# Selective scan: the first x unit of each group projected two slots ahead, the z rows in slots six and seven

## What is computed

```python
def _ssd_branch(h, w_in, conv_w, conv_b, dt_bias, A, d_skip, norm_w, w_out, h0_f, h0_b, with_out):
    proj = h @ w_in                       # z | x | B | C | dt
    z, rest = proj[..., :D_INNER], proj[..., D_INNER:]
    xbc = silu(_dwconv(rest[..., :CONV_DIM], conv_w, conv_b))      # five taps along the tokens
    xs, bm, cm = ...                      # x: 4 groups x 8 heads x 64; B, C: 4 groups x 128
    dt = softplus(rest[..., CONV_DIM:] + dt_bias)
    y_f, s_f = _ssd_scan(xs, dt_f, A[0], bm, cm, h0_f, with_out)   # chunks of 128 tokens
    y_b, s_b = _ssd_scan(flip(xs), flip(dt_b), A[1], flip(bm), flip(cm), h0_b, with_out)
    y = y_f + flip(y_b) + d_skip * xs
    gy = _rms_norm(y * silu(z), norm_w)   # per group of 512 channels
    return gy @ w_out, s_f, s_b
```

## Time and profile before

| | |
|---|---|
| median of 3 runs | 1860.78 us (1860.24 to 1864.98) |
| the profiled execution | 1859.74 us |
| its span, first to last instruction | 1857.9 us, and 1.8 us around it |
| mean granted PE clock | 0.994 of 2.4 GHz |
| PE, DVE, ACT, POOL busy | 97%, 61%, 49%, 5% of the span |
| first block of projections | 654.2 to 697.4 us of the span |
| round 0, 1, 2 | 697.4 to 761.4, to 827.8, to 893.2 us |
| experts | from about 1000 us to the end |

### The profile page before, as it was taken

One profiled execution on the slowest core, in us unless ns is written; L12 is line 12 of the kernel. 1 busy time (PEld: TensorE's weight loads), 2 busy tenths in 40 slices (PEclk: granted clock), 3 DMA queues, 4 the chain that ended last, 5 costly groups with the idle time before them and its releaser, 6 DMA issues.

```text
span 1857.9 us, 25616 instructions
## 1 busy us (share of the span) xinstructions
PE 1795.4 (97%) x10135; PEld 1316.4 (71%) x10136; DVE 1131.3 (61%) x1453; ACT 917.6 (49%) x1436; POOL 100.7 (5%) x81
## 2 busy tenths in 40 slices
PE   6989999999999999899999999999999999999997
PEld 5976788888888887687888566665666666655563
DVE  3266476765657797688867565565555555555644
ACT  3235573222246646577756455444454445444433
POOL 1000000000000123323300000000000000000000
PEclk9999999999999999999999999999999999999999
DMA  9466215666355532122259999999999999999995
GB/s 355 146 212 243 91 46 182 211 196 201 139 193 193 164 94 69 37 78 68 92 190 355 386 390 407 409 412 414 410 407 411 412 413 409 409 412 412 413 407 239
DMA packets 182459, 498.22 MB, mean 268 GB/s; under 512 B 10348, under 2 KB 62908, under 8 KB 167996
## 3 DMA queue, kind: packets, MB, share of 16 engines
q1 hardware_dynamic: 181760, 495.93, 70.6%
q10 hardware_dynamic: 571, 0.57, 0.1%
HBM read 495.42 MB, written 1.05 MB: 267 GB/s over the span
## 4 chain that ended last, share of the span: by engine, by line
PE 77%; DVE 8%; DMA 5%; ACT 4%; SPq 3%; issue 2%; POOL 0%; ACTq 0%; DVEq 0%; POOLq 0%
PE bank L991 12%; PE bank L992 11%; PE bank L993 11%; PE bank L1681 9%; PE bank L1673 4%; PE bank L1256 4%; PE bank L1258 4%; PE bank L1257 4%; DMA raw<-in_moe_gu_w_dram 3%; SPq L854 2%; DVE ar L3045 2%; PE bank L1356 2%; PE bank L1357 2%; PE bank L1358 2%; SPq L849 1%
## 5 line engine op out<-in xcount | busy, mean ns | idle before, releaser
L2685 DVE TENSOR_TENSOR lo<-raw,hi 128x1024 fp32r<-128x1024 f32 x182 | 216.9, 1222 | 171.1 <-ACT hi L1975 169.0
L2666 DVE TENSOR_TENSOR lo<-raw,hi 128x1024 fp32r<-128x1024 f32 x172 | 212.8, 1243 | 146.8 <-ACT hi L1955 144.5
L1955 ACT ACTIVATE hi<-raw 128x1024 fp32r<-128x1024 f32 x156 | 164.7, 1059 | 259.1 <-PE bank L1258 172.7
L1975 ACT ACTIVATE hi<-raw 128x1024 fp32r<-128x1024 f32 x182 | 187.0, 1057 | 146.5 <-DMA raw<-in_moe_gu_w_dram 55.5
L991 PE MATMUL bank<-hi,xg_t 128*128 128x512 f32 x448 | 182.3, 407 | 3.4 <-ACT ar L2488 1.4
L992 PE MATMUL bank<-lo,xg_t 128*128 128x512 f32 x448 | 175.2, 391 | 0.0
L993 PE MATMUL bank<-hi,xg_t 128*128 128x512 f32 x448 | 174.9, 390 | 0.0
L2685 DVE TENSOR_TENSOR lo<-ar,hi 128x1024 fp32r<-128x1024 f32 x94 | 112.1, 1222 | 90.4 <-ACT hi L1975 89.1
L991 PE MATMUL bank<-hi,hth 128*128 128x512 f32 x400 | 160.1, 400 | 2.0 <-DVE lo L2685 1.9
L992 PE MATMUL bank<-lo,hth 128*128 128x512 f32 x400 | 156.0, 390 | 0.0
L993 PE MATMUL bank<-hi,htl 128*128 128x512 f32 x400 | 155.8, 390 | 0.0
(11 more groups left out here) (400 smaller groups left out, 3328.9 us busy)
## 6 DMA issues: line engine op xcount, KB each, us to landing
raw<-in_moe_gu_w_dram SPq DMA_DIRECT2D x126, 1024.0 KB, 16.0
raw<-in_moe_down_w_dram SPq DMA_DIRECT2D x60, 1024.0 KB, 16.3
ar<-in_moe_gu_w_dram SPq DMA_DIRECT2D x59, 1024.0 KB, 17.9
out_slot<-in_moe_gu_w_dram SPq DMA_DIRECT2D x39, 1024.0 KB, 15.6
ar<-in_moe_down_w_dram SPq DMA_DIRECT2D x33, 1024.0 KB, 16.1
raw<-in_ada_w_dram SPq DMA_DIRECT2D x14, 2048.0 KB, 9.1
raw<-in_ffn_gu_w_dram SPq DMA_DIRECT2D x22, 1024.0 KB, 5.2
raw<-in_ffn_down_w_dram SPq DMA_DIRECT2D x22, 1024.0 KB, 4.9
```

The costliest lines, as they stand in the source:

```text
L1955: A_(hi[:, p % SPL, :], raw[:, slot(u), (p % 2) * PIECE:(p % 2 + 1) * PIECE], ACT.Copy).then_inc(hi_ready, 1)
L1975: A_(hi[:, q % SPL, :], m_raw(i)[:, (q % 2) * PIECE:(q % 2 + 1) * PIECE], ACT.Copy).then_inc(m_hi, 1)
L2666: TT(lo[:, p % SPL, :], raw[:, u, h * PIECE:(h + 1) * PIECE], hi[:, p % SPL, :].bitcast(F32), ALU.subtract).then_inc(done, 1)
L2685: TT(lo[:, q % SPL, :], src[:, (q % 2) * PIECE:(q % 2 + 1) * PIECE], hi[:, q % SPL, :].bitcast(F32), ALU.subtract).then_inc(m_lo, 1)
```

## The change

Nothing is computed differently. For groups 1, 2 and 3 the two pieces of the first x unit move from slots 0 and 1 to slots 8 and 9 of the round (or block) in front. z of group 1 and group 2 goes as two whole units into slots 6 and 7, two pieces in each. ACT takes the first x unit from the banks in slot 0 and not in slot 1, and z in slots 7 and 8 and not in 7 and 9, ahead of `conv_out` in slot 8. DVE's convolutions of the first x unit stand in slots 1 and 2, those of the second in 4 and 5 as before. `used_by` follows. The fillers of slot 9 of the first block and three of four groups of three in slots 7 to 9 of round 0 go away. Round 3 is as it was.

```diff
         def used_by(g, k):
 
+            ahead = max(0, k - 8)
             if g < 0:
-                return 2 * S_GRP + min(k, 6)
-            if g == 0:
-                return 2 * S_GRP + 6 + min(k, 6)
-            a = 2 * S_GRP + 12 + 10 * (g - 1)
-            if g < N_GROUPS - 1:
-                return a + k
-            return a + min(k, 4) + max(0, k - 6)
+                return 2 * S_GRP + min(k, 6) + ahead
+            a = 2 * S_GRP + (8 if g == 0 else 14 + 10 * (g - 1))
+            if g == N_GROUPS - 1:
+                return a - 2 + min(k, 4) + max(0, k - 6)
+            return a + min(max(0, k - 2), 4) + (2 * min(max(0, k - 6), 2) if g > 0 else 0) + (ahead if g < N_GROUPS - 2 else 0)
@@ PE, project(g, k) @@
                 if k < 4:
-                    proj("x", g, k // 2, k % 2)
+                    if g == 0 or k >= 2:
+                        proj("x", g, k // 2, k % 2)
                 elif k < 6:
                     proj("bc", g, 0, k - 4)
-                elif g > 1:
-                    proj("z", g - 1, (k - 6) // 2, k % 2)
-                if k == 9 and g == 0:
-                    fill(bank[2][:, 0:256], 3)
+                elif k < 8:
+                    if g > 1:
+                        for h in range(2):
+                            proj("z", g - 1, k - 6, h)
+                elif g + 1 < N_GROUPS:
+                    proj("x", g + 1, 0, k - 8)
                 if k >= 5:
                     to_tok(g, k - 5)
                 if k == 9:
-                    if g == 0:
-                        fill(bank[2][:, 0:256], 3)
                     cb(g)
@@ PE, scan(g, k) @@
                 project(g + 1, k)
-                if g == 0 and k >= 7 or g == N_GROUPS - 1 and k in (4, 5):
+                if g == N_GROUPS - 1 and k in (4, 5):
                     late_fill(g, 3)
@@ ACT, project(g, k) @@
-                for i in {1: (0, 1), 3: (2, 3), 5: (4, 5), 8: (6, 7)}.get(k, ()):
+                if k in (7, 8) and g > 1:
+                    zs(g - 1, k - 7)
+                for i in {(0 if g > 0 else 1): (0, 1), 3: (2, 3), 5: (4, 5), 8: (6, 7)}.get(k, ()):
                     if i >= 2:
                         conv_out(g, i - 2)
                     if i < 6:
                         conv_in(g, i)
-                if k in (7, 9) and g > 1:
-                    zs(g - 1, (k - 7) // 2)
@@ DVE, project(g, k) @@
-                if 2 <= k <= 7:
-                    conv(g, k - 2)
+                at = (2, 3, 4, 5, 6, 7) if g == 0 else (1, 2, 4, 5, 6, 7)
+                if k in at:
+                    conv(g, at.index(k))
```

## The result

The changed kernel takes **1908.74 us** (median of 4 runs, 1907.61 to 1910.06) where the kernel before takes 1862.43 (1860.24 to 1864.98, 4 runs beside it): a ratio of **1.0256**, with an interval of 1.0244 to 1.0269. Its profiled execution took 1907.61 with a span of 1905.8; against the span before, 1857.9, that is +47.9 us. The mean granted clock fell from 0.994 to 0.982.

A forecast was written before the change was run, and what follows sets the result against it. Slot by slot, PE's own work or the chain of DVE's, ACT's and PE's short steps, whichever ends last, bounds it. 3.7 - 0.2 + 24.2 - 0.2 + 13.5 = 41.0 us on 1859.74 gives 1902, range 1884 to 1914.

The forecast's parts named there:

- The first block: Slots 8 and 9 get two x pieces in place of fillers and waits; start of round 0 +6.0 us.
- the start chain: ACT's queue ahead of `state_out` at a round's start: PE idles some 6 us in round 0, 10 in rounds 1 and 2.
- The waits for z's copy: Rounds 1 and 2: PE's second z unit or next x waits for ACT's copy behind `m_`, three times, 4 to 5 us.
- if L1356 does not wait for L2273: Sign of being wrong: in the changed profile PE's projection is not held by ACT's copy out of bank 0.
- The rest of round 1: Slots 6 to 9: +24.2 us, of it 11 x pieces, 9.6 the two waits, 3.1 their clock.
- the clock term: Low clock after idling: 1.6 us charged for each long wait of PE, 9.9 us in the sum.
- The start of round 1: From round's start to first `yy` 21.4 us, before 21.6: -0.2 us, the whole 11 us saved given back.
- the rest of round 2: Slots 6 to 9: z waits in slot 7, copy, Silu and table load precede `conv_out` in slot 8; +13.5 us.
- (a): Rival: only round starts and added x bind, ACT's z copies come early enough; +14 us, 1875; 7%.
- (b): Rival: faster, x pieces fill PE's gaps at a round's end and the start chain is not exposed; -14 us, 1847; 4%.
- (c): Rival: PE stays cold, the low clock covers more of each restart; 10 to 15 us more, about 1914; 16%.
- (d): Rival: no change, work is only reordered and the waits found are hidden by the queue; 3%.

The follow-up runs named there:

- e10: Kernel before with only the first x unit of groups 1 and 2 moved ahead, z as before; 1868.43 us, ratio 1.0037.
- e8: e7 with PE projecting slot 2's x piece ahead of `late` and `bc`; 1866.19 us, ratio 1.0025.
- e11: e8 with z one piece a slot in round 2 and DVE's convolutions back in slots 2 to 7; 1855.04 us, ratio 0.9964.
- e1: Changed kernel with ACT's two z copies moved from slots 7 and 8 to 6 and 7, Silu left in slot 8; 1886.53 us, ratio 1.0132.
- e9: Changed kernel with 11 fillers (round 0) and 22 (rounds 1 and 2) in PE's wait ahead of `state_lat`; 1902.49 us, ratio 1.0222.
- e3: Changed kernel with 18 fillers (round 0) and 36 (rounds 1 and 2) ahead of `state_lat`, longer than the wait; 1914.73 us, ratio 1.0279.
- e7: e1 with ACT running two `conv_in` and one `state_out` ahead of the first `ce_` at a round's start; 1872.89 us, ratio 1.0063.
- e4: Kernel before with both z pieces of a unit in slots 6 and 7, ACT's copies in 7 and 8, no x moved; 1889.23 us, ratio 1.0149.

## Why the prediction was right, and where it was not

It forecast slower, 1902 us in a range of 1884 to 1914, and 1908.74 was measured. Against the profiled executions it was +41.0 forecast and +47.9 measured.

**The steps that held.** The first block ran 6.4 us longer for 6.0; so close a hit is luck, since that mark scatters by up to 3.5 us. PE waits for `state_out` 5.3 us in round 0 and 10.1 in rounds 1 and 2; the prediction had "some 6" and 10. That e10 gains nothing from a round with an x unit less at its start, and that e8 and e11 save 7 to 9 of the 11 us a round once ACT's and PE's order are changed, shows that the start chain, and not DVE's or ACT's sum, took the gain. The waits for z's copy came three times at 4.5 to 4.9 (4.6 forecast), and e1 shows the copy as their cause although the profile named another. By its letter the prediction's sign of being wrong ("if L1356 does not wait for L2273") was met in that trace; only e1 set it aside. The Silu ahead of `conv_out` in round 2 cost a wait of 6.4 us; in round 1 it was covered by the x piece. The rest of round 1 was 23.6 for 24.2 (the parts that the prediction gives for it in brackets sum to 23.7; its steps give the 24.2). SP, POOL and the experts gave nothing back, as costed.

**The terms that were sized too small** are those of a round's start, and the largest is the clock term, 1.6 us for each long wait, taken from one z piece at 4.45 in place of 2.88. At a round's start the low clock covers `state_lat`, `late` and `bc`, and e9 and e3 put it at 2.4 to 2.5. The start of round 1, from the timelines of after and e9, by its terms: `state_lat` begins 12.56 us after the round's start, forecast 11.9, because the gated multiply on DVE ahead of `seg` took 2.00 us there and 1.23 before (+0.7); from `state_lat` to `yy` at the full clock 8.5 us and not 7.9 (+0.6); the low clock 2.4 and not 1.6 (+0.8). Together +2.1, the whole gap between 23.5 and 21.4. Round 2 has the same +2.2, and round 0, which has no gated multiply, +1.0 of it.

Why that multiply took longer can be read from the traces. Before (first row) it ran alone. In the changed kernel POOL's product (L945) runs beside it:

```profile
763.23 1.23 DVE L3122 TENSOR_TENSOR ar<-ar,raw 128x1024 f32<-128x1024 f32 x1
```

```profile
768.59 2.00 DVE L3123 TENSOR_TENSOR ar<-ar,raw 128x1024 f32<-128x1024 f32 x1
```

```profile
768.46 1.04 POOL L945 TENSOR_TENSOR ar<-ar 128x512 f32<-128x512 f32 x1 [6.12 <-PE bank L1419]
```

POOL waits there for PE's `state_ctx`, which begins 0.6 us after a round's start now that no x piece stands ahead of it, and began at 6.0 before. So the move itself made the two meet, and the prediction, which had POOL's products wait for ACT alone, did not see it. The count over all traces stands at the end. No run moved POOL's product by itself, so the cause rests on that count.

**In the rest of round 2** 1.8 us were missing. Behind the wait of 1.70 us in its slot 6 the prediction left the clock whole, as it had been before. Afterwards it fell there too, as in round 1, and the z piece that starts at 906.75 took 4.44 us where the one at 873.94 of the kernel before took 2.96: 1.5 of the 1.8. That is chance as far as the traces tell, since in e1 the clock stayed whole at the same place. The windows view of PE alone, changed kernel:

```profile
907.00:909.00 2.00, 2.00 (x12) 0.53 0.00 0
909.00:911.00 2.00, 2.00 (x13) 0.62 0.00 0
```

**Sum of the misses:** round 0 +1.6 (0.4 at its start), round 1 +2.1 and -0.6, round 2 +2.2 and +1.8: 7.1, and 41.0 + 7.1 = 48.1.

**The rivals.** (a), only starts and added x bind, with 1875: its condition, the copy ahead of `m_`, is what e1 makes, and e1 takes 1886.5, +24.8 for +14. The rest of round 1 is then +11.0, as (a) has it. What it lacked is the wait of 5.8 us for the Silu and its table load in round 2, whose rest is +7.1 for 0, and the size of the starts (+3.3 us in rounds 1 and 2 together, for -0.4); the two waits of 10 us were in its sum. The Trainium skill, "Perfetto Trace Analysis", Optimizing Tensor Performance, asks that independent matmul groups rotate through PSUM banks, so that the copy out of one overlaps the next. e1's trace agrees that the copy held up the second unit (4.47 us in round 1, gone in e1), but no run here has a third bank, and for this wait the copy's place on ACT was enough. (b), faster, decided by `state_out` within about 1.5 us of the round's start: e7, e8 and e11 bring it to 2.5 us, and that alone was not enough; only e11, with PE's and DVE's order changed and z single in round 2, is faster, by 5.7 us where (b) had 14, as the first block and the z pairs of round 1 still cost. (c), the clock stays low for longer: half right. The clock was under-sized, by 0.5 to 1.0 us a wait at the starts; filling all three of those waits with work gives back 6 us of the time (8 of the rounds' lengths), not the 10 to 15 that (c) wanted beyond the forecast. (d), no change, is refuted by 46 us.

**What each part is worth**, as far as runs tell: z pairs alone +27.5 (e4), the first x of groups 1 and 2 alone +7.7 (e10). That leaves 11 us of the 46 for what only the two together bring, presumably group 3's x pieces in round 1 (11 us of PE's time that round 2 does not give back) and their wait. That remainder is a difference, and no run shows it by itself.

## What to carry to other kernels

Work moved off the start of a round shortens it only if the chain that the work had covered is short; so write that chain out, engine by engine and in each engine's program order, before counting on the gain. When a producer is moved, move the step that empties its PSUM bank with it: here the copy's slot on ScalarE, not any engine's busy time, was worth 22 us. And an operation that can run before the chain's first link (here `state_out` and two `conv_in`) belongs ahead of it in its engine's order. Ask also what a step that now comes sooner will run beside: here POOL's product met a VectorE multiply on the chain, which took 2.00 us in place of 1.23.

## What the runs showed of the hardware

The granted clock of 0.50 behind an idle wait of 10.1 us lasted some 5 us into PE's work (from 779.34 to between 783 and 785) and cost 2.4 us.

A wait of about 1.7 us of PE can be followed by the low clock or not, at the same place of the program. The wait for ACT's L2248 in slot 6 of rounds 1 and 2, 1.70 to 1.92 us long, stands 24 times in 12 of the 13 traces (e8's two are 1.59 and 1.46 us long, with the clock whole behind both); the granted clock fell to 0.50 within 2 us behind 13 of them and stayed 1.00 behind 11. It fell in round 1 of the kernel before (807.55) and not in its round 2 (873.94); in the changed kernel it fell in both (814.76 and 906.75), and in e1 only in round 1, not in round 2 (893.57). The z piece behind it took 4.4 us in place of 2.9. What decides it was not tested.

An f32 filler of 256 columns has two records in the timeline: 22 of them are x44 and took 9.66 us, 0.44 each. A matmul of the z projection with as many columns takes 0.12 (24 in 2.9 us).

A VectorE multiply of 128x1024 f32, from two operands, took longer whenever a GpSimd product ran beside it. The gated multiply stands 52 times in the 13 traces, four in each. Of these 18 have POOL's product of 1.04 us beside them, begun 0.13 us earlier, and took 1.98 to 2.00 us; the other 34 have none and took 1.22 to 1.23. The 18 are those of rounds whose first x unit had moved away, and only those.
